# One loop for all rounds of the expert stage on TensorE and ScalarE

## What is computed

```
def hier_moe(xn, ...):      # first block
    ...
    top_v, top_i = lax.top_k(e_in_group, TOP_K_INNER)        # 2 of 32 experts for each token
    gates = g_prob * jax.nn.softmax(top_v, axis=-1)
    ...
    hdn = lax.ragged_dot(xs, w_e_in, group_sizes)            # each expert: 1024 -> 2 x 256
    gate_h, up_h = jnp.split(hdn, 2, axis=-1)
    act = jax.nn.silu(gate_h) * up_h
    ys = lax.ragged_dot(act, w_e_out, group_sizes)           # 256 -> 1024
    ys = ys * gates...
    return jnp.zeros_like(xt).at[tok_sorted].add(ys)
...
mem_kv = mem_n @ w_mem_kv[layer]                             # second block, its first product
```

## Time and profile before

| | |
|---|---|
| median of 3 runs | 1370.04 us (1368.72 to 1370.3) |
| the profiled execution | 1366.27 us |
| its span, first to last instruction | 1364.5 us |
| mean granted clock of PE in it | 0.981 |
| PE busy in matmuls | 1249.6 us, 92% |
| ACT, POOL, DVE busy | 633.8, 781.1, 500.2 us |
| HBM traffic over the span | 201 GB/s |

### The profile page before, as it was taken

How to read it: one execution, slowest core, us unless ns; L and a number is a source line. 1 busy time by engine, 2 the same in 40 slices (tenths; PEclk the granted TensorE clock), 3 DMA queues, 4 the chain that set the end, 5 groups by cost and what they waited for, 6 DMA issues and landing times.

```text
span 1364.5 us, 19503 instructions
## 1 busy us (share of the span) xinstructions
PE 1249.6 (92%) x7839; PEld 1026.0 (75%) x7839; DVE 500.2 (37%) x1040; ACT 633.8 (46%) x1093; POOL 781.1 (57%) x347
## 2 busy tenths in 40 slices
PE   6999999898887876998999999999999889899997
PEld 5888877776342332877779999888997777899986
DVE  4629743343121112345623223202468271322211
ACT  6345534643111012635646555446797442655551
POOL 6769986440000001874047988788689804888884
PEclk9899999999999999998999999999999999899999
DMA  6645554377999999543015655544535403355551
GB/s 237 201 140 184 192 179 154 143 302 280 422 422 417 419 422 391 186 154 108 1 35 191 207 186 185 200 164 176 185 124 185 178 25 123 126 185 185 186 188 74
DMA packets 126116, 275.12 MB, mean 202 GB/s; under 512 B 7445, under 2 KB 53837, under 8 KB 113741
## 3 DMA queue, kind: packets, MB, share of 16 engines
q1 hardware_dynamic: 125328, 272.71, 54.6%
q10 hardware_dynamic: 700, 1.21, 0.3%
HBM read 272.85 MB, written 1.05 MB: 201 GB/s over the span
## 4 chain that ended last, share of the span: by engine, by line
PE 75%; DMA 7%; ACT 7%; DVE 5%; POOL 3%; issue 2%; ACTq 0%; SPq 0%; DVEq 0%
PE lin_ps L900 12%; PE lin_ps L902 11%; PE lin_ps L901 11%; PE lin_ps L920 8%; PE lin_ps L922 8%; PE lin_ps L923 8%; DMA ring<-in_w_expert_in 4%; PE sc_ps L1164 3%; POOL w_low L831 3%; DMA work<-in_w_expert_out 2%; ACT w_high L1446 2%; PE lin_ps L1181 2%; PE lin_ps L1006 2%; PE sc_ps L975 2%; PE lin_ps L1149 1%
## 5 line engine op out<-in xcount | busy, mean ns | idle before, releaser
L831 POOL TENSOR_TENSOR w_low<-ring,w_high 128x1024 fp32r<-128x1024 f32 (+1 forms) x320 | 772.4, 2452 | 566.7 <-ACT w_high L1446 566.7
L1446 ACT ACTIVATE w_high<-ring 128x1024 fp32r<-128x1024 f32 (+1 forms) x320 | 312.2, 1040 | 138.5 <-PE lin_ps L902 99.1
L920 PE MATMUL lin_ps<-x_high,w_high 128*128 128x256 f32 x960 | 272.8, 284 | 0.0
L922 PE MATMUL lin_ps<-x_high,w_low 128*128 128x256 f32 x960 | 271.8, 283 | 0.0
L923 PE MATMUL lin_ps<-x_low,w_high 128*128 128x256 f32 x736 | 208.4, 283 | 0.0
L920 PEld LDWEIGHTS lin_ps<-x_high,w_high 128*128 128x128 f32 x960 | 184.5, 192 | 0.1
L922 PEld LDWEIGHTS lin_ps<-x_high,w_low 128*128 128x128 f32 x960 | 184.5, 192 | 0.1
L900 PE MATMUL lin_ps<-w_high,x_high 128*128 128x512 f32 (+1 forms) x432 | 170.9, 396 | 2.6 <-POOL w_low L831 2.6
L901 PE MATMUL lin_ps<-w_low,x_high 128*128 128x512 f32 (+1 forms) x432 | 168.7, 390 | 0.0
L902 PE MATMUL lin_ps<-w_high,x_low 128*128 128x512 f32 (+1 forms) x368 | 143.7, 391 | 0.0
L923 PEld LDWEIGHTS lin_ps<-x_low,w_high 128*128 128x128 f32 x736 | 141.4, 192 | 0.0
(11 more groups left out here) (400 smaller groups left out, 1943.0 us busy)
## 6 DMA issues: line engine op xcount, KB each, us to landing
ring<-in_w_expert_in SPq DMA_DIRECT2D x31, 2048.0 KB, 14.6
ring<-in_ffn_w_in SPq DMA_DIRECT2D x44, 1024.0 KB, 7.4
ring<-in_w_in SPq DMA_DIRECT2D x14, 2048.0 KB, 7.8
ring<-in_b_w_in SPq DMA_DIRECT2D x11, 2048.0 KB, 8.0
work<-in_w_expert_out SPq DMA_DIRECT2D x8, 2048.0 KB, 23.6
ring<-in_w_expert_out SPq DMA_DIRECT2D x8, 2048.0 KB, 17.6
ring<-in_ffn_w_out SPq DMA_DIRECT2D x8, 2048.0 KB, 8.0
ring<-in_a_w_in SPq DMA_DIRECT2D x4, 2048.0 KB, 8.0
```

Of the source, the lines that this page charges most:

```text
L831: pool.tensor_tensor(w_low[:, slot, 0:words], raw, w_high[:, slot, 0:words].bitcast(F32), ALU.subtract).then_inc(low_made, 1)
L920: pe.matmul(out, wh[:, j, at], high(k), start=(k == 0 and f < 2), stop=False, skip_group_check=True)
L922: pe.matmul(out, wl[:, j, at], high(k), start=False, stop=False, skip_group_check=True)
L1446: act.activation(w_high[:, slot, 0:words], raw, ACT.Copy).then_inc(high_made, 1)
```

## The change

PE and ACT have one loop each over the pairs of batches of all rounds. Its end is a value in a register, `n_rounds * (BATCHES // 2)`. The Ifs and the second copies of the pair go. A pair computes the same numbers as before: with `it = 2 * pair + parity` counted over all rounds, the semaphore counts that it waits for are those that the round and the pair gave before. PE still writes out batches 0 and 1.

```
-            def expert_pair(r, pair):
+            def expert_pair(pair):
                 for parity in range(2):
-                    it = r * BATCHES + 2 * pair + parity
-                    expert_batch(it, r * (BATCHES // 2) + pair, parity, 32 * it + 16)
+                    it = 2 * pair + parity
+                    expert_batch(it, pair, parity, 32 * it + 16)
...
             expert_batch(1, 0, 1, 48, extra=True)
-            with pe.Fori(1, BATCHES // 2) as pair:
-                expert_pair(0, pair)
-            with pe.If(n_rounds > 1):
-                with pe.Fori(1, n_rounds) as r:
-                    with pe.Fori(0, BATCHES // 2) as pair:
-                        expert_pair(r, pair)
+            with pe.Fori(1, n_rounds * (BATCHES // 2)) as pair:
+                expert_pair(pair)
...
-            def expert_round(r):
-                with act.Fori(0, BATCHES // 2) as pair:
-                    for parity in range(2):
-                        b = 2 * pair + parity
-                        it = r * BATCHES + b
-                        act.wait_ge(moe_gate_t, it + 1)
+            def expert_pair(pair):
+                for parity in range(2):
+                    it = 2 * pair + parity
+                    act.wait_ge(moe_gate_t, it + 1)
...
-                        act.wait_ge(expert_used[2 + parity], r * (BATCHES // 2) + pair + 1)
+                    act.wait_ge(expert_used[2 + parity], pair + 1)
...
-            expert_round(0)
-            with act.If(n_rounds > 1):
-                with act.Fori(1, n_rounds) as r:
-                    expert_round(r)
+            with act.Fori(0, n_rounds * (BATCHES // 2)) as pair:
+                expert_pair(pair)
```

More of the change, by code:

```diff
@@ L1602, in _ @@
             act.activation(small[:, 14:16], small[:, 12:14], ACT.Exp).then_inc(router_exp, 1)
-            def expert_round(r):
-                with act.Fori(0, BATCHES // 2) as pair:
-                    for parity in range(2):
-                        b = 2 * pair + parity
-                        it = r * BATCHES + b
-                        act.wait_ge(moe_gate_t, it + 1)
[L1610 to L1616, removed]
-                        act.wait_ge(expert_used[2 + parity], r * (BATCHES // 2) + pair + 1)
-                        act.activation(y_slots[:, NB:2 * NB], y_ps[:, 1, :], ACT.Copy).then_inc(moe_y_moved, 1)
+            def expert_pair(pair):
+                for parity in range(2):
+                    it = 2 * pair + parity
+                    act.wait_ge(moe_gate_t, it + 1)
+                    act.activation(gates_T, moe_tr_ps[:, 0:SEQ], ACT.Copy).then_inc(moe_gate_moved, 1)
+                    act.wait_ge(expert_used[1], it + 1)
+                    act.activation(silu_out, hid_ps[:, 0:D_EXPERT], ACT.Silu).then_inc(moe_silu, 1)
+                    act.wait_ge(moe_act_t, it + 1)
+                    act.activation(act_T, moe_tr_ps[:, SEQ:2 * SEQ], ACT.Copy).then_inc(moe_act_moved, 1)
+                    act.wait_ge(moe_y_half, it + 1)
+                    act.activation(y_slots[:, 0:NB], y_ps[:, 0, :], ACT.Copy).then_inc(moe_y_moved, 1)
+                    act.wait_ge(expert_used[2 + parity], pair + 1)
+                    act.activation(y_slots[:, NB:2 * NB], y_ps[:, 1, :], ACT.Copy).then_inc(moe_y_moved, 1)
```

## The result

| | before | changed |
|---|---|---|
| runs of the result | 1368.62 us median of 10 (1362.79 to 1370.3) | 1360.16 us median of 10 (1356.17 to 1364.7) |
| the profiled execution, its span | 1366.27, 1364.5 us | 1358.77, 1357.1 us |
| mean granted clock of PE in it | 0.981 | 0.984 |

The ratio is 0.9946, 95% interval 0.9931 to 0.9961. The direction was right, the forecast signs at the exit show in the trace, and the figure was off: 1360.16 us lies 1.6 us under the range (1361.8 to 1368.0).

A forecast was written before the change was run, and what follows sets the result against it. PE was taken to bound the kernel, busy 92% of 1364.5 us. From 1370.04 us, 3.3 (idle at the loop's exit) and 2.5 (clock), together 5.8, gave 1364.2 us; range 1361.8 to 1368.0.

The forecast's parts named there:

- the forecast signs at the exit: L1205 gone, `kv00` starting after 0.4 to 0.6 us, released by POOL, clock at 1.00, no instruction packet in between.
- The exit: PE's loop exit: without the If and its jump, `kv00` starts at 543.0 instead of 546.29, 3.3 us (bounds 0 and 3.8).
- The clock: PE behind the loop's exit: no fall to half clock, `kv00` takes 11.5 us instead of 14.0, 2.5 us (bounds 0, 2.7).
- Rival A: PE behind the loop's exit: the clock falls all the same, only 3.3 us remain, 1366.7 us; chance 10%.
- The premise that an idle under 2.6 us is safe: PE in the expert stage: an idle of 2.58 us left the clock alone, only one of 5.07 slowed the 32 matmuls.
- POOL's supply and the carrying on: `kv00` and `kv01`: POOL's units are ready for an earlier PE, tightest by 0.5 to 0.7 us; the whole gain carries on.
- The loop test and ACT: PE's loop passes: register compare under 0.1 us more, hidden by a wait; ACT's If takes 50 ns, so nothing from either.
- The rule of the skill: Instruction fetch, against the change: prefetch is purely sequential; a taken branch outside the resident two pages forces a fetch.
- rival B: PE's loop exit: a fetch is paid anyway, or L1205 waited for something else; about 1370.0 us; chance 8%.
- The sum: Whole kernel: 3.3 us at the exit plus 2.5 us of clock, 5.8 us.
- the last of the sum: Whole kernel: 5.8 us taken from the median of the runs shown, 1370.04, not the profiled 1366.27, giving 1364.2 us.
- my case: Whole kernel: the forecast itself, 1364.2 us, from 1362 to 1366.5; chance 79%.

The follow-up runs named there:

- run 3: Kernel before, with four matmuls instead of the second copy inside PE's If: ratio 0.9961, the branch 215 ns.
- run 5: Kernel before, with the second copy of the pair twice in a row inside PE's If: the branch 6267 ns; ran once, no ratio.
- run 4: Kernel before, with one batch instead of a pair inside PE's If, a jump over 284 records: the branch 342 ns; no ratio.
- run 6: Changed kernel plus a never-taken If around 284 matmuls on PE behind the attention over a window, where DMA engines are nearly idle: ratio 0.9981, 1364.57 us.
- run 9: Both kernels unaltered, timed again: the changed one 0.9959, 1361.83 us; the kernel before against itself 0.9987, 1366.73 us.
- run 2: Kernel before with the change on ACT alone, PE keeping its If and second copy: ratio 1.0003, the branch 6233 ns.
- run 1: Kernel before with the change on PE alone, ACT keeping its If and second copy: ratio 0.9956, 1360.45 us.
- run 7: Changed kernel, PE held ahead of `kv00` until POOL made low parts of three units (1.0008, 1367.14 us) or two (idle 2.77 us, no ratio).
- run 8: Changed kernel plus an If ending each pass of PE's loop, around 284 never-run matmuls (0.9996, 1366.25 us) or 1024 (no ratio).

## Why the prediction was right and wrong

**The exit.** Right to the tenth: 3.25 us of idle against 3.3 forecast (PE's start moved by 2.9 only, since the stage ended 0.34 later). The cause is a fetch of instructions at a jump's target: 0.2 us for a short jump (run 3), 6.3 for the far ones (run 5), 0.3 where the next packet holds the target (run 4), 3.7 with idle DMA engines (run 6).

**The clock.** Right in the profiled pair, 2.42 us against 2.5. As a constant it was too firm: stalls of 3.4 to 3.8 us at the exit were followed by half the clock for 6.8 us in three profiles (before, run 5 and run 9's of the kernel before) and for 3.4 us in run 2, where `kv00` took 564.03 - 551.08 = 12.95 us, so this term is 1.4 to 2.6 (for run 5 once its second wait of 1.84 us is taken off its 15.70). Rival A did not occur in the three profiles with the change (the result's, run 1 and run 9's). The premise that an idle under 2.6 us is safe does not hold (run 7); the forecast idle of 0.5 us did not depend on it. That the idle alone does it is shown by run 7.

**POOL's supply and the carrying on.** Right: PE came to the transposes of `u0` at 563.16 instead of 568.50, and the gain of 5.33 us at `kv01` was still there at the end of the span, with 2.1 more.

**The loop test and ACT.** Right: PE's back jumps 220 and 245 ns; the change on ACT alone 1.0003.

**The rule of the skill and rival B.** The code behind the loop was there after each back jump, and the back jumps themselves cross 2.2 packets in 254 ns at most, so the strict reading of "Instruction fetch mechanics" in the Trainium skill, Runtime: NRT & Kernel Launch, does not hold on PE. Its other half, that a far taken branch waits for a fetch, does, and run 5 adds that the branch waits no longer for a farther target.

**The sum.** 5.8 us was forecast and 6.2 (standard error 0.65) is measured over all runs, 5.6 by the second timing (0.9959 of 1367). The two profiled spans differ by 7.4 us because one of them holds the stretch at 606 us; the ratio 0.9946 comes to 7.4 us too, but whether its runs had that stretch is not known. That stretch, or one like it between 606 and 626 us, shows in four of the five profiles with an idle over 3 us at the exit (before, runs 5, 7 with three units, 9; not run 2) and in one of the nine others (run 8 with 1024 matmuls). So it may go with an idle at the exit; that is a count over single executions, why is open, and no run was made to separate it.

**The step that failed** is the last of the sum: "the median of the runs shown is 3.8 above it, and on that footing I predict". The profiled execution (1366.27) was near the kernel's usual time, the median of 1366.9 over 105 runs; the three runs (1368.72 to 1370.3) were not. Of the 4.0 us by which 1364.2 was too high, 3.1 are this base (1370.04 against 1366.9), 0.6 a gain of 6.4 by the medians of all runs instead of 5.8, and 0.3 that the ten runs of the result lie under the median of all 21. With the result's own ten runs of the kernel before (1368.62) the split would be 1.4 for the base and 2.7 for the gain; the larger number of runs is the better judge. Subtracting from the profiled execution, where the terms had been measured, gives 1360.5, and 1360.16 was measured. That it comes so close is partly luck: 1366.27 lies 0.6 below the usual time and the gain about as much above 5.8. The range failed with it: 1362 to 1366.5 for my case allowed for one stretch at half clock more or less, while runs of one and the same program lie over 8 to 13 us. That spread goes with the clock: over 95 runs of the kernel before that list it, time and mean granted clock correlate at -0.86, 1.2 us for each 0.001 of clock. An estimate agrees: 0.001 less in the mean over 1365 us is 2.7 us at half clock, which cost PE 1.4 us if it is at work.

## What to carry to other kernels

Code that does not run still costs if the jump over it lands beyond the instruction packet in use and the next one, in a packet that no earlier pass has fetched. On TensorE the branch took 3.7 us with idle DMA engines and 5.9 to 6.3 with busy ones; the array stood for 2.8 to 3.8 us of that, with half the clock for 3.4 or 6.8 us behind it. Look for a compare-and-branch of several microseconds in the sequencer's records where the profile says "issue" or names an engine that had been ready; merge the loops so that the common way falls through, or keep what stands in the If short. And take a forecast's base from many runs, or from the execution in which its terms were measured.

## What was not expected of the hardware

- The far jump costs 6267 ns over 567 records and 6267 ns over 1134, each at the exit of the same loop with the DMA engines full; another one, with them idle, 3748. The difference lies before the packet moves (3.6 us against 1.0); from there to the branch's end it is 2.5 to 2.7 us in all seven profiles.
- A loop on PE keeps its code over a distance of 2615 records if most of these were never fetched: back jumps of 214 and 252 ns.
- The same idle is not always followed by the same clock: 2.77 us brought it down for 3.4 us in run 7 and for 6.8 in run 6, 3.73 for 3.4 in run 2 and 3.74 for 6.8 in run 5, and a wait of 2.6 us at one place of the program did nothing in the kernel before and cost 3.4 us of half clock in run 7.
